# Adding the experts' results to their tokens' rows in DRAM by an indirect DMA

## What is computed

```python
def _moe_swiglu(h, w_router, b_router, w_gate, w_up, w_down):
    ...                                   # top 2 of 8 experts per token, softmax gates
    def expert_block(args):
        xb, e = args
        g = jax.nn.silu(xb @ w_gate[e])
        return (g * (xb @ w_up[e])) @ w_down[e]
    ...                                   # each token: sum of gate * expert result
h = h + _moe_swiglu(hn, ...)
```

## Time and profile before

| | us |
|---|---|
| median of 3 runs | 4295.19 |
| lowest, highest run | 4279.59, 4298.38 |
| span of the profiled execution, first to last instruction | 4306.3 |
| time of one steady job | 91.75 |
| the eight jobs, from the first gate/up product to the last add | 3548.59 to 4283.38 |

### The profile page before, as it was taken

One profiled execution on the slowest core, in us unless ns is written; L12 is line 12 of the kernel. 1 busy time (PEld: TensorE's weight loads), 2 busy tenths in 40 slices (PEclk: granted clock), 3 DMA queues, 4 the chain that ended last, 5 costly groups with the idle time before them and its releaser, 6 DMA issues. The chain is left out here.

```text
span 4306.3 us, 57009 instructions
## 1 busy us (share of the span) xinstructions
PE 4030.0 (94%) x22187; PEld 3386.2 (79%) x22187; DVE 1556.6 (36%) x2751; ACT 1339.6 (31%) x2314; POOL 224.2 (5%) x187
## 2 busy tenths in 40 slices
PE   8998899999999989999998889999999879999999
PEld 6777786787777878678776777877776759999998
DVE  2265544332326554433233554333325421111121
ACT  3374443331336544323233233322223311111111
POOL 0150100000006010000000000000001000000000
PEclk9998989999999989999999899999999779999999
DMA  3100011222210001122211002222221015555544
GB/s 125 44 1 1 0 39 65 92 89 67 70 59 1 1 0 36 62 88 98 69 69 54 1 1 78 82 99 83 85 86 43 20 67 198 203 204 186 214 169 147
DMA packets 54649, 333.51 MB, mean 77 GB/s; under 512 B 7600, under 2 KB 8496, under 8 KB 23520
## 3 DMA queue, kind: packets, MB, share of 16 engines
q1 hardware_dynamic: 51904, 324.95, 21.3%
q0 software_dynamic: 2592, 6.49, 0.6%
HBM read 326.17 MB, written 4.19 MB: 77 GB/s over the span
## 5 line engine op out<-in xcount | busy, mean ns | idle before, releaser
L501 PE MATMUL bank<-high 128*128 128x512 f32 x2480 | 973.7, 393 | 46.6 <-DVEq L591 30.2
L502 PE MATMUL bank<-low,high 128*128 128x512 f32 x2480 | 971.4, 392 | 0.0
L503 PE MATMUL bank<-high,low 128*128 128x512 f32 x2480 | 971.2, 392 | 0.0
L501 PEld LDWEIGHTS bank<-high 128*128 128x128 f32 x2480 | 469.7, 189 | 151.8 <-DVEq L591 34.3
L503 PEld LDWEIGHTS bank<-high,low 128*128 128x128 f32 x2480 | 469.3, 189 | 98.4
L502 PEld LDWEIGHTS bank<-low,high 128*128 128x128 f32 x2480 | 469.6, 189 | 97.8
L561 DVE TENSOR_TENSOR low<-weight_ring,high 128x2048 fp32r<-128x2048 f32 (+1 forms) x144 | 319.2, 2218 | 586.8 <-ACT high L518 586.8
L3163 PE MATMUL bank<-chosen,glu_ring 128*128 128x176 f32 x2816 | 424.2, 313 | 0.0
L3163 PEld LDWEIGHTS bank<-chosen,glu_ring 128*128 128x128 f32 x2816 | 421.0, 190 | 0.0
L518 ACT ACTIVATE high<-weight_ring 128x2048 fp32r<-128x2048 f32 (+1 forms) x144 | 266.7, 1853 | 266.1 <-PE bank L503 227.0
L239 PE MATMUL bank<-filler 128*128 128x512 f32 x1031 | 290.3, 428 | 18.5 <-PEq L172 11.8
(11 more groups left out here) (514 smaller groups left out, 4762.3 us busy)
## 6 DMA issues: line engine op xcount, KB each, us to landing
glu_ring<-in_w_expert SPq DMA_DIRECT2D x88, 1024.0 KB, 4.8
weight_ring<-in_w_ff SPq DMA_DIRECT2D x64, 1024.0 KB, 5.0
down_ring<-in_w_expert_down SPq DMA_DIRECT2D x64, 704.0 KB, 5.1
weight_ring<-in_w_in SPq DMA_DIRECT2D x22, 1024.0 KB, 4.8
weight_ring<-in_w_ffe SPq DMA_DIRECT2D x22, 1024.0 KB, 4.8
weight_ring<-in_w_downe SPq DMA_DIRECT2D x16, 704.0 KB, 4.1
weight_ring<-in_w_ino SPq DMA_DIRECT2D x11, 1024.0 KB, 4.9
weight_ring<-in_w_ine SPq DMA_DIRECT2D x9, 1024.0 KB, 4.9
```

Source lines behind the costliest of these rows:

```text
L501: nc.tensor.matmul(mem.bank[b][:, :], whole, high[:, k, :], start=(k == 0), stop=False)
L502: nc.tensor.matmul(mem.bank[b][:, :], whole, low[:, k, :], start=False, stop=False)
L503: last = nc.tensor.matmul(mem.bank[b][:, :], rest, high[:, k, :], start=False, stop=(k == kt - 1))
```

## The change

- `token_rows` gets 176 spare rows, and there is a second DRAM tensor of the same size, `sum_rows`. In `route`, POOL clears a tile `zeros`, and SP stores it to the spare rows of both and to all of `sum_rows`: 8 DMAs, ahead of the four that store the tokens.
- A slot with no token now names a spare row of its own (the constant `token` is the token number less 1024, and DVE adds 1024 and takes the minimum with `spare`).
- In the jobs the transposes of `picks`, `spreader`, `rows_high`, `rows_low`, the spread and the adds to `mem.x` are gone. ACT writes the gated rows to `out_rows`, float32, in the same place in its order, and first waits until the last job's scatter has landed. POOL then issues two indirect DMAs that add the 2x88 rows to `sum_rows` (`scatter`), and waits for them to land before it takes up the next job.
- Behind the jobs a new phase, `add_rows`, loads `sum_rows` in four DMAs of 512 KB into `tokens`, turns it on TensorE (32 transposes, behind 12 filler products) and adds it to `mem.x` on DVE (8 adds).

```diff
@@ route
         @block.sync
             sp.dma_start(router[:, :], a["router"]).then_inc(loaded, 16)
             sp.dma_start(bias[:, :], a["router_b"].partition_broadcast(P)).then_inc(loaded, 16)
+            sp.wait_ge(cleared, 1)
+            for s in range(BLOCK_TILES):
+                spare = slice(SEQ + s * height, SEQ + (s + 1) * height)
+                sp.dma_start(token_rows[spare, :], zeros[0:height, :]).then_inc(zeroed, 16)
+                sp.dma_start(sum_rows[spare, :], zeros[0:height, :]).then_inc(zeroed, 16)
+            for t in range(TT):
+                sp.dma_start(sum_rows[t * P:(t + 1) * P, :], zeros[:, :]).then_inc(zeroed, 16)
...
             sp.wait_ge(stored, 16 * TT)
+            sp.wait_ge(zeroed, 16 * (TT + 2 * BLOCK_TILES))
+        @block.gpsimd
+            nc.gpsimd.memset(zeros[:, :], 0.0).then_inc(cleared, 1)
@@ new, called behind run_jobs
+def add_rows(nc, mem, tokens, sum_rows):
+    parts = KD // 2
...
+        @block.sync
+            for c in range(parts):
+                at = slice(c * width, (c + 1) * width)
+                sp.dma_start(tokens[:, :, at], sum_rows[0:SEQ, at].rearrange("(t p) d -> p t d", p=P)) \
+                    .then_inc(loaded[c], 16)
+        @block.tensor
+            fill_in(nc, mem, mem.bank[KD - 1], 12)
+            for k in range(KD):
+                if k % 2 == 0:
+                    pe.wait_ge(loaded[k // 2], 16)
+                for t in range(TT):
+                    last = nc.tensor.transpose(mem.bank[k][:, t * P:(t + 1) * P], tokens[:, t, k * P:(k + 1) * P],
+                                               CONST(mem.const, "ident"))
+                last.then_inc(turned, 1)
+        @block.vector
+            for k in range(KD):
+                dve.wait_ge(turned, k + 1)
+                nc.vector.tensor_tensor(mem.x[:, k, :], mem.x[:, k, :], mem.bank[k][:, :], ALU.add)
@@ run_jobs, tensor
-                for s in range(BLOCK_TILES):
-                    for t in range(TT):
-                        last = nc.tensor.transpose(high[s][0:height, t * P:(t + 1) * P], picks[:, t, parts[s]],
-                                            CONST(mem.const, "ident"))
-                    last.then_inc(turned, 1)
                 pe.wait_ge(picked_out, j * pairs + pairs)
                 for u in range(EXP_T):
-                    if u < EXP_SLOTS:
-                        pe.wait_ge(added, j * KD + (KD - EXP_SLOTS + u + 1))
...
                     if u == EXP_SLOTS - 1:
                         pe.wait_ge(picks_ready, j + 2)
+                        pe.wait_ge(rows_ready, j * turns + turns)
                         index()
-                pe.wait_ge(turned_out, j * turns + BLOCK_TILES)
...
-                pe.wait_ge(picked_out, j * pairs + 2 * pairs)
-                for k in range(KD):
...
-                        for part, rows in enumerate((rows_high, rows_low)):
-                            last = nc.tensor.matmul(low[k % EXP_SLOTS][:, :], rows[0:height, s, k * P:(k + 1) * P],
-                                                    spreader[0:height, s, :], start=(s == 0 and part == 0),
-                                                    stop=(s == BLOCK_TILES - 1 and part == 1))
-                    last.then_inc(spread, 1)
@@ run_jobs, gpsimd
+            pool.sem_inc(landed, 1)
+            def scatter(j):
+                pool.wait_ge(slot_ready, j + 1)
+                pool.wait_ge(rows_ready, j * turns + 2 * turns)
+                pool.sem_inc(begun, 1)
+                for s in range(BLOCK_TILES):
+                    nc.gpsimd.indirect_dma_start(
+                        sum_rows, bass.IndirectOffsetOnAxis(ap=slot_token[0:height, s:s + 1], axis=0),
+                        out_rows[0:height, s, :], None, compute_op=ALU.add).then_inc(scattered, 16)
             def job(j):
                 pool.wait_ge(picked, j * pairs + pairs)
                 gather(j * BLOCK_TILES + BLOCK_TILES)
+                scatter(j)
+                pool.wait_ge(scattered, j * (16 * BLOCK_TILES) + 16 * BLOCK_TILES)
+                pool.sem_inc(landed, 1)
@@ run_jobs, scalar
-                act.wait_ge(turned_out, j * turns + BLOCK_TILES)
+                act.wait_ge(landed, j + 1)
                 gated_rows(j, 0)
                 take_picked(j * pairs + pairs)
                 gated_rows(j, 1)
@@ run_jobs, vector
                 dve.wait_ge(index_ready, j * BLOCK_TILES + BLOCK_TILES)
+                dve.wait_ge(rows_ready, j * turns + turns)
...
                     if u == EXP_SLOTS - 1:
+                        dve.wait_ge(landed, j + 1)
+                        nc.vector.tensor_copy(slot_token[0:height, :], next_token[0:height, :]) \
+                            .then_inc(slot_ready, 1)
+                        dve.wait_ge(slot_ready, j + 1)
                         take_index(j * BLOCK_TILES + BLOCK_TILES)
...
-                for k in range(KD):
-                    dve.wait_ge(spread, j * KD + (k + 1))
-                    dve.wait_ge(added, j * KD + (k + 1))
-                    nc.vector.tensor_tensor(mem.x[:, k, :], mem.x[:, k, :], low[k % EXP_SLOTS][:, :], ALU.add) \
-                        .then_inc(added, 1)
```

More of the change, by code:

```diff
@@ L2863, in lay_out_second, with route @@
     lay_out_odd(i, a)
-def route(nc, mem, a, tokens, token_rows, job_key, job_gate, job_expert, job_count):
-    with buffers(nc, router=[P, KD * N_EXPERTS], by_token=[P, SEQ], bias=[P, N_EXPERTS], logits=[P, TT, N_EXPERTS],
+def route(nc, mem, a, tokens, token_rows, sum_rows, job_key, job_gate, job_expert, job_count):
+    with buffers(nc, zeros=[P, D_MODEL], router=[P, KD * N_EXPERTS], by_token=[P, SEQ], bias=[P, N_EXPERTS], logits=[P, TT, N_EXPERTS],
                  best=[P, TT, 8], place=[P, TT, 8], part=[P, TT, 2], hot=[P, TT, 2, N_EXPERTS],
@@ L3048, in mixture, with _, run_jobs @@
         rms_norm(nc, mem, mem.x, gain, mem.h, ahead=[(mem.moe_const[:, :], a["moe_const"])])
[L3049 to L3054, removed]
+        route(nc, mem, a, tokens, token_rows, sum_rows, job_key, job_gate, job_expert, job_count)
+        run_jobs(nc, mem, a, token_rows, sum_rows, job_key, job_gate, job_expert, job_count)
+        add_rows(nc, mem, tokens, sum_rows)
+def add_rows(nc, mem, tokens, sum_rows):
+    parts = KD // 2
+    with phase(nc, *[f"loaded{c}" for c in range(parts)], "turned") as (block, *sems):
+        loaded, turned = sems[:parts], sems[parts]
+        width = D_MODEL // parts
+        @block.sync
+        def _(sp):
+            for c in range(parts):
[3 more added lines that the diff above has]
+        @block.tensor
+        def _(pe):
+            fill_in(nc, mem, mem.bank[KD - 1], 12)
[7 more added lines that the diff above has]
+        @block.vector
+        def _(dve):
+            for k in range(KD):
+                dve.wait_ge(turned, k + 1)
+                nc.vector.tensor_tensor(mem.x[:, k, :], mem.x[:, k, :], mem.bank[k][:, :], ALU.add)
+def run_jobs(nc, mem, a, token_rows, sum_rows, job_key, job_gate, job_expert, job_count):
+    pairs, turns = KD // 2, 2 * BLOCK_TILES
     height = BLOCK // BLOCK_TILES
@@ L3057, in run_jobs @@
     names = [f"glu_filled{s}" for s in range(EXP_SLOTS)] + [f"down_filled{s}" for s in range(EXP_SLOTS)]
-    names += ["picks_ready", "indexed", "index_ready", "begun", "gathered", "picked", "picked_out", "glu_product", "silu_ready", "hidden_ready", "down_product",
-              "down_out", "turned", "high_rows", "turned_out", "spread", "added"]
+    names += ["picks_ready", "indexed", "index_ready", "begun", "gathered", "picked", "picked_out", "glu_product",
+              "silu_ready", "hidden_ready", "down_product", "down_out", "turned", "rows_ready", "slot_ready", "scattered", "landed"]
     glu_size = 2 * KD * P
@@ L3062, in run_jobs @@
                  gates=[P, TT, 2], rows=[P, BLOCK_TILES, D_MODEL], chosen=[P, KD, BLOCK], silu=[P, EXP_SLOTS, BLOCK], hidden=[P, EXP_T, BLOCK],
[L3063 to L3064 removed]
+                 result=[P, KD, BLOCK], slot_gate=[P, BLOCK_TILES], next_gate=[P, BLOCK_TILES],
+                 out_rows=[P, BLOCK_TILES, D_MODEL]) as (
+            glu_ring, down_ring, picks, gates, rows, chosen, silu, hidden, result, slot_gate, next_gate, out_rows), \
+            nc.sbuf_tensor(f"next_token_{nc.next_id()}", [P, BLOCK_TILES], U32) as next_token, \
             nc.sbuf_tensor(f"slot_token_{nc.next_id()}", [P, BLOCK_TILES], U32) as slot_token, \
[L3066 to L3067 removed]
             phase(nc, *names) as (block, *sems):
         glu_filled, down_filled = sems[:EXP_SLOTS], sems[EXP_SLOTS:2 * EXP_SLOTS]
[L3070 to L3071 removed]
+        (picks_ready, indexed, index_ready, begun, gathered, picked, picked_out, glu_product, silu_ready, hidden_ready,
+         down_product, down_out, turned, rows_ready, slot_ready, scattered, landed) = sems[2 * EXP_SLOTS:]
         halves = [slice(h * SEQ, (h + 1) * SEQ) for h in range(2)]
@@ L3221, in _ @@
         def _(act):
+            act.sem_inc(rows_ready, turns)
```

(11 more changed lines are left out.)

40 lines of the change are left out of this document (14 added, 26 removed).

## The result

| | us |
|---|---|
| before, median of 4 runs (lowest, highest) | 4296.55 (4279.59, 4298.38) |
| after, median of 4 runs (lowest, highest) | 4256.43 (4242.39, 4260.97) |
| ratio, 95% interval | 0.991 (0.9885 to 0.9934) |
| the profiled execution of after: its time, its span | 4260.97, 4259.2 |
| a second set of the kernel after, 5 runs: median, ratio | 4253.99, 0.9909 (0.9892 to 0.9927) |

Faster by 40.1 us, 0.9%; the forecast was 46.4. The page of after answers to the earlier trace rows: TensorE's share is as high as it was, with less of it.

A forecast was written before the change was run, and what follows sets the result against it. TensorE's own work was taken as the bound, PE busy 94% of the span. Joints -57.9, job 0 -1.0, scatter and route 0, tail +12.5 sum to -46.4 us: from 4295.2 to 4249 us, range 4229 to 4274.

The forecast's parts named there:

- The joints: Between the 8 jobs: spread and transposes of picks leave PE's stream, 8.27 us at each of 7 joints, 57.9 us.
- (a): Rival: a new wait at the joints costs 2 us a job, 14 in all, giving 4263 us; chance 0.15.
- (b): Rival: the spread hid the weight loads, so jobs keep 91.75 us and the kernel takes 4307; chance 0.05.
- (d): Rival: the granted clock falls at each joint, losing 3 us each, giving 4270 us; chance 0.01.
- Job 0: Start of the first job: its first product comes 1.0 us sooner, without the transposes at half clock.
- The scatter in the jobs: Adding transfers inside the jobs: cost 0, landing may be as late as G + 38, cover 30 us thick.
- L: Time the adding transfers take to land, counted from the second scatter's issue; taken as 5 us.
- G: The new start of the next job's gate/up products, from which the scatter's issue and landing are counted.
- route: Added POOL memset and 8 zero stores, 3.5 MB, ahead of the token stores: cost 0, at most 3 us.
- The tail: Behind the last job: landing, end of phase, loads, transposes and adds end 12.5 us later than before.
- The last norm: Final norm begins with PE at half clock before and after: cost 0, bounds -3 and +3.5 us.

The follow-up runs named there:

- scatter_x3: The new kernel with each job's scatter done three times, each behind the last one's landing; median 4323.18 us, ratio 1.0085.
- same_phase: The new kernel with add_rows' loads moved into the jobs' phase, behind a POOL semaphore, and 40 fillers instead of 12; median 4246.06 us, ratio 0.9887.
- plain_scatter: The new kernel with the scatter a plain write instead of an add; median 4252.50 us, ratio 0.9911.
- before_zeros: The old kernel plus the memset and the eight stores of zeros in route; ratio 1.0004 over 10 runs.
- no_scatter: The new kernel with no scatter at all, route, gated rows and add_rows kept; median 4238.16 us, ratio 0.9877.
- scatter_x6: The new kernel with each job's scatter done six times, each behind the last one's landing; median 4564.07 us, ratio 1.063.
- no_fill: The new kernel without the 12 filler products of add_rows; median 4251.20 us, ratio 0.9885.

## Why the prediction was right, and where it was not

- **The joints.** Forecast 8.27 us each, measured 8.17 in the changed kernel, and the same job length without any scatter. Rivals (a), (b) and (d) did not happen: PE's wait is 0.30 us, the weights are there, the clock is 1.00. The missing 0.1 is the first product behind a wait. The spread's first product lasted 0.49 us and the later ones 0.39 to 0.40; now a gate/up product is the first, with 0.41 us against 0.31, and the four units take 19.36 us for 19.26. So 0.1 us of what went had to be paid again, and the branch on PE costs nothing that the trace shows.
- **Job 0.** Forecast 1.0 beside its joint's 8.27, measured 7.5 for both, from the gather's landing to job 1's first product (96.65 us before, 89.17 after). Of the missing 1.8, some 1.5 us are a clock that came back later, 8.0 us behind the first turns instead of 5.6, behind 0.64 us of idle that the old kernel did not have. The first product itself came 0.85 us sooner behind the turns, close to the forecast.
- **The scatter in the jobs.** Forecast 0 with 30 us of cover. 0 it is, but L was mis-sized here too: with the weight loads that begin 5.2 us behind G, the second scatter of a job lands 10 to 11 us behind its issue (10.5 at the first joint) and not 5; with the plain scatter it was 4.8 to 5.2 there. The landing is at G + 14 and the cover 24 us thick. The point that the cover ends at was right: in `scatter_x3` DVE went on at G + 42.1 and PE waited 3.5 us, so it lies at G + 38.6, for G + 38 forecast.
- **`route`.** Forecast 0; by itself a ratio of 1.0004, no cost that the runs can tell.
- **The tail** is the term that was mis-sized: 12.5 forecast, 18.7 measured. Counted from ACT's last rows: POOL's adding instructions take 1.6 us each, where the gather's 0.98 was put (0.65 late at the second issue); L was 7.2, not 5 (+2.2); and 3.9 us stand between landing and first load, where 0.8 was put (+3.1). That last step took the price of a phase's end from a place where POOL had arrived long before; its DRAIN was in the old trace, 7.52 us long from 4213.6, beside the products of the last job. The first part's landing was 5.8 us, not 3.9 (in `same_phase` 3.6, so the cause is open), but the end by DVE's adds came to 12.0 us behind the first load's issue as against 11.8. From the last turn of job 7 to the last add are 27.3 us, where the forecast had some 21. The Trainium skill ("DMA: Bandwidth & Descriptors", the anatomy of one DMA; "Collectives: The Full Stack", why ReduceScatter is half of AllGather) leads to an estimate of 5.3 us for L, and of 3.7 without the add. The measured 7.2 and 4.8 agree in the direction, an add is dearer, and are each longer.
- **The last norm** gave 3.1 us back (sums in 7.13 us, 10.04 before), at the lower bound. In both executions of the kernel after and in `plain_scatter` the sums took 7.13, in the old kernel and in `before_zeros` 10.04 and 10.07, and in `no_scatter`, with the same `add_rows` ahead of the norm, 8.83, each behind the same 2.4 us of idle. Why the clock held in some and fell in others is open. That these 3.1 us belong to the change is not shown; they are luck for the forecast, which would have lain 3 us further off without them.

Sum: the forecast -46.4 became -40.8. The six later joints gave 0.6 less, job 0 with its joint 1.8 less, the tail cost 6.2 more, and the norm gave 3.1 back. The median of 4256 lies 7 us above 4249.

## What to carry to other kernels

If TensorE is the bound and never waits, work taken from its stream comes back almost in full at each joint (here 8.17 us of 8.27), and what replaces it elsewhere is free until its latency passes the next point that waits for it; work that point out in us before anything else. The part to distrust is the serial end behind the last iteration: count every hand-over there, the leaving engine's own end of phase included. An engine that was always early at a barrier has an exit cost that lies off the path in the earlier trace, but it stands there: look it up in the list of the phase's end. And where a wait of TensorE is added, it can cost more than its length, by the clock.

## What the hardware showed that I had not expected

- POOL's DRAIN at the end of a phase in which it issued indirect DMAs before: 2.84 us behind an adding and a plain scatter, with the transfers already landed. The length is not fixed: 2.76 us in `scatter_x6`, 5.45 in `scatter_x3`, and 7.2 to 7.5 us in the old kernel and in `no_scatter`, where it stands right at two gathers that POOL has not waited for. What it depends on is open. Other engines go on meanwhile if they need no barrier.
- An indirect DMA that adds holds POOL for 1.6 us against 1.0, and the second of two (0.72 MB together) lands 7.2 us behind its issue against 4.8 on an empty queue. Beside 1 MB weight loads a pair takes 12 to 13 us from the first issue to the last landing, and 9.1 in the tail.
- Four 512 KB loads issued together: the first lands 5.8 us behind its issue in the kernel after, 3.6 in `same_phase`, 4.7 in `no_fill`. What made them differ is open.
- Waits of 3.51 and 3.56 us in the same place, in two jobs of `scatter_x3`: behind the first TensorE's clock stayed at 1.00, behind the second it was at 0.50.
